# A two-block hybrid layer on one core: first transfers, last group norm, down projection and tail reordered

## The reference

```
x   = rmsnorm(x) -> w_in (14336 columns) -> conv branch, S5 scan branch, gates -> w_o, residual
x   = rmsnorm(x, final_g)
u   = rms_norm(h, norm1_g);  proj = u @ w_in_2         # q,k,v and the RWKV columns
attn = dilated_attention(q, k, v)
y   = rwkv7 state recurrence over the 256 tokens, 16 heads of 64
y   = ((y - mu) * rsqrt(var + GN_EPS)) * ln_w + ln_b   # group norm, per head
rw  = (y + bonus) * g
h   = h + concat(attn, rw) @ w_out
u   = rms_norm(h, norm2_g)
h   = h + (silu(gate) * up) @ w_down                   # gate, up = u @ w_gate_up, 5632 wide
out = rms_norm(h, final_g_2)
```

## Time and profile before

| | |
|---|---|
| median of 3 runs | 2275.11 us (2267.45, 2275.11, 2280.07) |
| profiled execution | 2278.84 us, span 2277.1 us |
| busy: PE, PE weight load | 2218.3 us (97%), 2164.1 us |
| busy: DVE, ACT, POOL | 1570.3, 1035.5, 264.2 us |
| DMA | 387.81 MB, mean 170 GB/s |

### The profile page before, as it was taken

The page is one execution under the profiler, slowest core; times in us unless marked ns, Lnnn a source line. Parts: engine busy times, 40 slices in busy tenths (PEclk is TensorE's granted clock), DMA queues, the critical chain, the costliest instruction groups (busy, mean ns, idle before and its releaser), DMA issues.

```text
span 2277.1 us, 51586 instructions
## 1 busy us (share of the span) xinstructions
PE 2218.3 (97%) x20554; PEld 2164.1 (95%) x20554; DVE 1570.3 (69%) x2072; ACT 1035.5 (45%) x1341; POOL 264.2 (12%) x176
## 2 busy tenths in 40 slices
PE   7999999999999999999999999799999999999997
PEld 6999999999999989999999788699999999999997
DVE  6889998889545667768766677576666666654444
ACT  5544444444544445566344344554433334433442
POOL 0344444444100000100011000000000000000000
PEclk9999999999999999999999899999999999999999
DMA  7555555555555556555655011255555555556553
GB/s 249 172 170 183 177 177 178 178 185 187 185 187 189 185 197 193 183 174 176 203 176 181 30 49 58 66 185 185 186 185 187 187 184 185 185 171 190 185 181 131
DMA packets 106960, 387.81 MB, mean 170 GB/s; under 512 B 12016, under 2 KB 12144, under 8 KB 106608
## 3 DMA queue, kind: packets, MB, share of 16 engines
q1 hardware_dynamic: 104544, 377.36, 51.0%
q0 software_dynamic: 1888, 7.87, 1.0%
q10 hardware_dynamic: 432, 1.21, 0.1%
HBM read 384.29 MB, written 2.10 MB: 170 GB/s over the span
## 4 chain that ended last, share of the span: by engine, by line
PE 92%; DVE 5%; ACT 2%; issue 1%; DMA 1%; DVEq 0%; ACTq 0%
PE ps_main L1672 28%; PE ps_main L1674 27%; PE ps_main L1673 27%; PE ps_aux L1900 2%; DVE w_lo L968 2%; PE ps_main L1900 1%; PE ps_main L1971 1%; ACT w_hi L493 1%; PE ps_aux L1921 1%; PE ps_main L1973 0%; PE ps_main L1972 0%; PE ps_aux L1741 0%; PE ps_aux L1729 0%; DMA w_raw<-wmain 0%; PE ps_aux L1818 0%
## 5 line engine op out<-in xcount | busy, mean ns | idle before, releaser
L968 DVE TENSOR_TENSOR w_lo<-w_raw,w_hi 128x1024 fp32r<-128x1024 f32 x718 | 918.8, 1296 | 470.1 <-ACT w_hi L493 464.9
L493 ACT ACTIVATE w_hi<-w_raw 128x1024 fp32r<-128x1024 f32 x718 | 748.9, 1047 | 751.4 <-PE ps_main L1674 735.9
L1672 PE MATMUL ps_main<-xs,w_hi 128*128 128x256 f32 x1664 | 467.8, 281 | 2.7 <-DVE w_lo L968 1.8
L1673 PE MATMUL ps_main<-xs,w_hi 128*128 128x256 f32 x1664 | 464.5, 279 | 0.0
L1674 PE MATMUL ps_main<-xs,w_lo 128*128 128x256 f32 x1664 | 464.3, 279 | 0.0
L1672 PE MATMUL ps_main<-x3s,w_hi 128*128 128x256 f32 x1408 | 394.4, 280 | 0.0
L1674 PE MATMUL ps_main<-x3s,w_lo 128*128 128x256 f32 x1408 | 392.8, 279 | 0.0
L1673 PE MATMUL ps_main<-x3s,w_hi 128*128 128x256 f32 x1408 | 392.8, 279 | 0.0
L1672 PEld LDWEIGHTS ps_main<-xs,w_hi 128*128 128x128 f32 x1664 | 312.4, 188 | 9.5 <-DVE w_lo L968 5.4
L1674 PEld LDWEIGHTS ps_main<-xs,w_lo 128*128 128x128 f32 x1664 | 312.6, 188 | 0.0
L1673 PEld LDWEIGHTS ps_main<-xs,w_hi 128*128 128x128 f32 x1664 | 311.4, 187 | 0.0
(11 more groups left out here) (413 smaller groups left out, 3770.6 us busy)
## 6 DMA issues: line engine op xcount, KB each, us to landing
w_raw<-wmain SPq DMA_DIRECT2D x622, 512.0 KB, 3.4
w_raw<-wdown SPq DMA_DIRECT2D x80, 512.0 KB, 3.7
w_raw<-wdown SPq DMA_DIRECT2D x16, 256.0 KB, 2.7
bias<-bias POOLq DMA_DIRECT2D x8, 384.0 KB, 3.3
x_res<-xt POOLq DMA_DIRECT2D x4, 512.0 KB, 6.7
out<-x_res SPq DMA_DIRECT2D x4, 512.0 KB, 2.6
x_first<-xt SPq DMA_DIRECT2D x2, 512.0 KB, 5.9
x_first<-xt ACTq DMA_DIRECT2D x2, 512.0 KB, 9.4
```

The source lines that it names most:

```text
L493: nc.scalar.activation(whi[:, s, 0:width], raw[:, s, 0:width], ACT.Copy).then_inc(hi_ready, 1)
L968: V.tensor_tensor(wlo[:, s, 0:width], raw[:, s, 0:width], whi[:, s, 0:width].bitcast(F32), ALU.subtract)\
L1672: nc.tensor.matmul(out, whi[:, s, w], high[:, k, :], start=(first and kk == 0), stop=False)
L1673: nc.tensor.matmul(out, whi[:, s, w], low[:, k, :], start=False, stop=False)
```

## The change

The start: SP issues x piece 0, unit 0, x piece 2, unit 1, units 2 and 3, with no wait; constants and `c_raw` move to POOL's queue, behind a wait for the sum of squares on PE (`ssq_ready`), and `b_stage` stands behind them. ACT and DVE split unit 1 ahead of x pieces 2 and 3, and the squares and their sums move into the first two blocks of stage u.

The group norm: in the last chunk `group_out` of chunk 2 moves ahead of the copy of sa, and the halves of chunks 0 to 2 (`rwkv_high`, `rwkv_low`) ahead of the y copies. After the chunk, ACT makes the next weight split before it squares; DVE runs the last `group_out` ahead of the last two residual adds. PE enters woutb on `rwkv_ready` alone and asks for the two `wa_free` counts at the blocks that use those banks (the second and third).

The down projection starts on 42 blocks and asks for all 44 at the sixth unit of the first output block. In its loop ACT multiplies each finished block of x by final_g, in place, behind its square. The last square is summed by a second accumulating matmul on PE and not by DVE, and the end is five wide multiplications by the reciprocal root, stored in pieces of 4, 4, 4, 2 and 2 blocks.

```diff
@@ sync
             for c in (0, 2):
                 sp.dma_start(x0[:, 4 * c:4 * c + 4, :], x_dram[:, 4 * c:4 * c + 4, :]).then_inc(x_loaded[c], 16)
-            sp.wait_ge(x_loaded[0], 16)
-            for s in range(RING):
+                sp.dma_start(raw[:, c // 2, :], wmain[c // 2]).then_inc(w_loaded[c // 2], 16)
+            for s in (2, 3):
                 sp.dma_start(raw[:, s, :], wmain[s]).then_inc(w_loaded[s], 16)
-            sp.dma_start(const[:, :], const_dram).then_inc(const_loaded, 16)
-            sp.dma_start(craw[:, :, :, :], cst_dram).then_inc(c_loaded, 16)
@@ gpsimd
+            pool.wait_ge(ssq_ready, 1)
+            pool.dma_start(const[:, :], const_dram).then_inc(const_loaded, 16)
+            pool.dma_start(craw[:, :, :, :], cst_dram).then_inc(c_loaded, 16)
             scan_b(0)
@@ scalar
             raw_hi(1)
+            split_hi(At(1))
             raw_hi(2)
-            split_hi(At(1))
...
                 split_hi(At(n0 + 2 * b + 4))
+                if b < 2:
+                    squares(2 * b)
+                    squares(2 * b + 1)
...
                     rwkv_high(1, slice(0, 2 * CH))
+                    rwkv_high(2, toks(2))
...
+            wout_hi()
             square(NCH - 1)
             nc.scalar.activation(gg[:, 0:1], cst("eps"), ACT.Ln)
-            rwkv_high(2, toks(2))
-            wout_hi()
             act.wait_ge(gn_mm, 2 * NCH)
...
                     nc.scalar.activation(sq[:, 0, :], xj, ACT.Square).then_inc(sq_ready, 1)
+                    ins = nc.scalar.activation(xj, xj, ACT.Copy, scale=par_c("final2", j))
@@ vector
+                if last:
+                    group_out(i - 1)
                 mm("sa")
...
-                if i:
+                if i and not last:
                     group_out(i - 1)
...
                 if last:
+                    rwkv_low(1, slice(0, 2 * CH))
+                    rwkv_low(2, tokens(2))
                     mm("y")
...
             centre(NCH - 1)
+            wout_lo()
             wout_add()
+            group_out(NCH - 1)
             wout_lo()
-            rwkv_low(1, slice(0, 2 * CH))
-            rwkv_low(2, tokens(2))
+            rwkv_low(3, tokens(3)).then_inc(rwkv_ready, 1)
             wout_add()
-            wout_lo()
-            group_out(NCH - 1)
-            rwkv_low(3, tokens(3)).then_inc(rwkv_ready, 1)
+            wout_add()
             link(V.memset(acc[:, 0, :], 0.0))
-            wout_add()
...
-            for j in range(KB):
-                ins = V.scalar_tensor_tensor(x[:, j, :], x[:, j, :], par_c("final2", j), rstd[:, :], ALU.mult, ALU.mult)
+            dve.wait_ge(x_scaled, 1)
+            for j0, j1 in OUT_PIECES:
+                V.tensor_tensor(x[:, j0:j1, :], x[:, j0:j1, :], rstd[:, :].unsqueeze(1).to_broadcast([P, j1 - j0, L]), ALU.mult)\
+                    .then_inc(out_ready, 1)
@@ tensor
-            for b in range(2):
-                pe.wait_ge(wa_free[b], KB // 2)
             pe.wait_ge(rwkv_ready, 1)
...
+                if b < 4 and (g0 + b) % 4 < 2:
+                    pe.wait_ge(wa_free[(g0 + b) % 4], KB // 2)
...
-            pe.wait_ge(act_ready, FB)
+            pe.wait_ge(act_ready, FB - 2)
...
+                        if b == 0 and u == 5:
+                            pe.wait_ge(act_ready, FB)
...
-            norm_total(4, L)
+            pe.wait_ge(acc_ready, 3)
+            nc.tensor.matmul(aux[:, 3, 0:L], cst("ones"), acc[:, 0, :], start=True, stop=False)
+            pe.wait_ge(sq_ready, 3 * KB)
+            nc.tensor.matmul(aux[:, 3, 0:L], cst("ones"), sq[:, 0, :], start=False, stop=True).then_inc(norm_sum, 1)
```

More of the change, by code:

```diff
@@ L385, in _ @@
                           .then_inc(w_loaded[n.c % RING], 16)
-            for c in range(4):
+            for c, (j0, j1) in enumerate(OUT_PIECES):
                 sp.wait_ge(out_ready, c + 1)
-                sp.dma_start(out_dram[:, 4 * c:4 * c + 4, :], x[:, 4 * c:4 * c + 4, :]).then_inc(out_stored, 16)
-            sp.wait_ge(out_stored, 64)
+                sp.dma_start(out_dram[:, j0:j1, :], x[:, j0:j1, :]).then_inc(out_stored, 16)
+            sp.wait_ge(out_stored, 16 * len(OUT_PIECES))
         @block.gpsimd
@@ L517, in _, with squares @@
             raw_hi(1)
+            split_hi(At(1))
             raw_hi(2)
-            split_hi(At(1))
             raw_hi(3)
             split_hi(At(2))
-            for c in range(4):
+            def squares(c):
                 if c == 3:
@@ L948, in down @@
                     nc.scalar.activation(sq[:, 0, :], xj, ACT.Square).then_inc(sq_ready, 1)
+                    ins = nc.scalar.activation(xj, xj, ACT.Copy, scale=par_c("final2", j))
+                    if last and b == 3:
+                        ins.then_inc(x_scaled, 1)
             with act.Fori(0, 3) as i:
@@ L1052, in _ @@
                 lead(n0 + 2 * b)
+                if b == 0:
+                    squares_sum(1)
+                if b == 1:
+                    squares_sum(2)
+                    squares_sum(3)
+                    V.tensor_tensor(xsq[0][:, 0:2, :], xsq[0][:, 0:2, :], xsq[0][:, 2:4, :], ALU.add).then_inc(xsq_summed, 1)
                 if b == 3:
@@ L1640, in down @@
                     dve.wait_ge(sq_ready, j + (2 * KB + 1))
+                    if last and b == 3:
+                        break
                     evac(V.tensor_tensor(acc[:, 0, :], acc[:, 0, :], sq[:, 0, :], ALU.add), g)
                     dve.wait_ge(bank_free[g.c % 4], g.turns(4, 1))
+                    if last and b == 2:
+                        V.memset(tmp[:, 1, 0:1], 0.0).then_inc(acc_ready, 1)
             with dve.Fori(0, 3) as i:
```

14 lines of the change are left out of this document (5 added, 9 removed).

## The result

The changed kernel takes 2261.96 us (median of 7 runs, 2260.5 to 2268.6), the kernel before 2275.11 us on the same chip (7 runs). The ratio is 0.9947, with a 95% interval of 0.993 to 0.9965: 0.35 to 0.7% faster. The forecast was 2262.7 us with 12.4 us of gain; measured were 13.2 us between the medians, and by the interval anything from 8 to 16 us. The profiled execution took 2267.02 us, with a span of 2265.3 us, 11.8 us shorter than the span of before.

A forecast was written before the change was run, and what follows sets the result against it. TensorE is busy 97% of the span, so only its pauses, low-clock stretches and the two ends can yield; 4.0 + 4.8 + 2.4 + 1.2 = 12.4 us off the 2275.11 us median gives 2262.7 us, range 2254 to 2271.

The forecast's parts named there:

- A: Start: w0 loaded second, w1 split before x pieces 2 and 3, squares later; gain 4.0 us, bounds 0 and 6.0.
- B: Last group norm at the RWKV part's end: TensorE restarts 4.4 us earlier; with clock 4.8 us, bounds 2.2 and 6.3.
- The clock's part: After the pause ending the RWKV part: clock still falls, costing 1.5 us, 0.4 less than before.
- C: Down projection started on 42 of 44 blocks: the wait on the last activation goes; gain 2.4 us, bounds 2.2 and 2.4.
- D: Tail: final scale in the loop, five wide products, shorter last store; gain 1.2 us, bounds -0.3 and 2.0.
- (1): Rival: the start gives nothing, w1 late or squares in the norm chain's way; 2266.7 us, chance 13%.
- (2): Rival: chunk 2's norm gets in the way, so the group norm edit gives 2.2 us; 2265.3 us, chance 8%.
- (3): Rival: w1 lands at 12 us, no clock fall at the RWKV part's end; 15.9 us gained, 2259.2 us, chance 17%.
- Rival (4): Chunk stage: low clock held 30 us longer costs 15 us, making it slower at 2277.7 us; chance 5%.
- (5): Rival: last store or weight stream absorbs all gains; above 2270 us, chance 2%.

The follow-up runs named there:

- edit B alone: Kernel before with only the last group norm ahead of splits and residual adds, and wa_free waits at the second and third woutb blocks: 2270.44 us, ratio 0.9975.

## Why the prediction was right

**A, 4.0 us predicted, 4.2 to 4.7 us measured.** The weight tiles came as counted: w0's split at 8.22 (8.4 forecast), w1's at 12.87 (13.5). That the order "only swaps x piece 2 with w0" did not hold: x piece 2 landed at 10.76 us and not at about 12.3, but nothing waited for it. One step failed: "PE starts 2.37 us after the landing" took the same two instructions as before, but VectorE is now still at the low parts of x piece 0 and takes the tile at 9.87, so TensorE starts at 11.14 and not at 10.8. The chain took 2.92 us, 0.55 us more than counted, and the start came 0.34 us late; w1 landing 0.6 us earlier than counted gave it back, and the fourth unit came at 23.26 (23.7 forecast). The wait on x_raw_l was foreseen near 16 to 18 us and stood at 17.37. That the squares cost nothing behind the splits holds, and putting them back cost 2.55 us. This is more than the pause of before (1.97 us), since the pause on x_raw_l grew too (1.48 us against 1.11 us). The range is that of the profiles: the last xs piece stood at 65.33 to 65.54 us without the edit, and at 60.85 and 61.15 us in the two profiles of the changed kernel.

**B, 4.8 us predicted, 4.83 us measured in the first pair.** That the two agree to 0.03 us is luck: over the profiles the stretch took 40.4 to 40.9 us without the edit and 34.6 to 36.1 us with it, by the clock. The pause fell from 7.72 to 3.17 us (3.3 forecast), released by the last low half, and the third chunk's norm did not get in the way: the stack copy waited 0.23 us for TensorE behind it (0.2 us of slack forecast), and the longest such wait is 1.5 us as forecast. The clock's part was right in kind: it fell, and cost 1.5 us (34.57 us without a fall, 36.11 us with one), the number that was taken; before it cost 1.8 us by the same reckoning (7.80 us from the restart to the second addition against 5.96 us), and the 0.4 us that were credited for it were nearer 0.3 us. In the second profile there was no fall at all: both ends of that term occur with one kernel.

**C, 2.4 us predicted, 2.63 us measured** against runs whose clock stayed high, which is above the upper bound of 2.4. The term was read off the idle time, and that counts from the end of the last matmul's passage through the array. The starts of the two matmuls stood 2.65 us apart instead of 0.12, and the next one followed after 0.22 us instead of 0.12, which makes the 2.63 us:

```profile
2011.35 0.28 PE L1674 MATMUL ps_main<-x3s,w_lo 128*128 128x256 f32 x1
2014.00 0.38 PE L1672 MATMUL ps_main<-act,w_hi 128*128 128x256 f32 x1 [2.37 <-DVE act L988]
2014.22 0.28 PE L1673 MATMUL ps_main<-act,w_hi 128*128 128x256 f32 x1
```

The bound also rested on "the clock stayed high there", and it does not always: in the kernel with edit B alone the 2.4 us pause was followed by a fall, which cost another 1.4 us. Edit C takes away that risk too. Windows of that kernel:

```profile
2002.00:2004.00 2.00, 0.00 (x0) 0.97 0.74 199
2004.00:2006.00 2.00, 1.90 (x9) 0.50 0.16 64
```

**D, 1.2 us predicted, 0.86 us measured.** The reciprocal came 3.19 us behind the last addition (before 2.82 us, 3.06 forecast) and the products took 4.70 us (4.9 forecast), so VectorE was done when it should be. The mis-sized term is the last store, whose length was to be "nothing", less 0.1 us: it lands 3.11 us behind its issue, not 2.6 us, though it is half as long. Before, the four stores went out 1.6 us apart, moved 300 to 350 GB/s and took 2.6 us each; now five go out 0.6 to 1.1 us apart and fill the DMA engines, at some 400 GB/s:

```profile
2260.00:2261.00 1.00, 0.00 (x0) 0.00 (x0) 1.00 (x2) 0.00 (x0) 0.00 (x0) 0.50 1.02 410
```

(The numbers before the last three are the busy times of the five engines; the last three are the granted clock, the share of the DMA engines and GB/s.)

**The whole.** Predicted 12.4 us; the four stretches give 13.0 us in the first pair of profiles, 12.1 to 12.8 us edit by edit, and the medians 13.2 us. The mechanisms of all four terms are shown; that the sum lies within 1 us of the medians is closer than these runs can tell, whose interval is 8 us wide. Of the rivals, (1) falls with the last xs piece, 4.69 us earlier, (2) with the 0.23 us in front of the stack copy, (3) was near in one execution (no fall of the clock) but not in A. Rival (4), the clock of the chunk stage, named the right place for the wrong reason: that stage did cost 3.06 us more in the first profile, but it varies by as much without any edit (4.6 us between two profiles of the changed kernel), and it did not hold the low level 30 us longer. Its "later it was high" was misread: before, the clock was low a second time from 1272.6 us on, for 6.8 us. (5) falls with 2261.96 us.

## What to carry to other kernels

When a kernel keeps one engine busy for 97% of its span, list that engine's pauses and ask of each which instructions of the other engines stand in front of its releaser for no reason; orders cost nothing to change, and here four of them gave 13 us. Compare such a change by stretches between the same events of two profiles, and check that a stretch that no edit touches has kept its length: here the untouched ones moved by up to 3 us, as much as an edit. The cost of a pause is the distance of the starts around it, which the idle time alone understates (2.63 against 2.37 us). A gap filled with work that must be repeated is not filled; letting the first instructions of the blocked work wait for their own operand alone gave the same 1 us for one more wait.

## What the runs showed of the hardware

The clock of TensorE differed between executions of one program at the same place. Behind the pause of 3.17 us it fell in five of the six profiles that have it, and of the two profiles of the changed kernel in one; behind the 2.4 us pause it fell in one kernel of four; at the start of the chunk stage it was low for 6.8, 10.2, 13.6 or 20.5 us, which made that stage 169.6 to 175.9 us long. The mean granted clock of a run is a guide to this: runs of the kernel before at 0.991 had spans of 2277.5 to 2280.3 us, most of those at 0.995 had 2271 to 2272 us.

It is not the whole guide. Among the runs of the kernel before at a mean clock of 0.994 or 0.995, eleven had spans of 2261.6 to 2266.2 us and the 36 others 2269.7 to 2274.0 us: about 9 us apart at the same clock. No profile of a short run was taken, and what makes the two groups is open.

TensorE has two steady paces for the wide matmuls with the clock at 1.00, 0.1178 and 0.1133 us. The faster one is in every profile: between 960 and 1030 us, in six stretches of 5.2 us and one of 21.5 us in most profiles, and further on in stretches of 10.7 us between the attention's small matmuls (near 1160, 1200 and 1240 us in the changed kernel's first profile, near 1180 and 1220 us in its second). In the first profile of the changed kernel each of them lies between matmuls of another form. Others come and go with the execution: near 138 to 158 us in three profiles and 155 to 163 us in a fourth, and all of woutb in one. They sum to 76 to 106 us a profile, 136 us with that woutb. A group of runs that is 9 us shorter would need some 230 us more of them, so that they make the two groups is not shown.
